# Down-projection with four accumulators instead of seven, its shared products summed in PSUM

## The reference

```python
    hn2 = rmsnorm(x, norm2_g[l])
    up, ffn_new = causal_dwconv(hn2 @ w_up[l], st_ffn[l], ffn_conv_w[l])
    a_f, b_f = jnp.split(up, [D_FF], axis=-1)
    x = x + (jax.nn.silu(a_f) * b_f) @ w_down[l]
y = rmsnorm(x, norm_f_g)
```

## Time and profile before

| | us |
|---|---|
| median of 3 runs | 3172.16 (3170.81 to 3173.29) |
| the profiled execution | 3174.32 |
| its span, first to last instruction | 3172.60 |
| PE busy in the span | 3123.2 |
| DVE busy | 2001.3 |
| ACT busy | 833.6 |
| POOL busy | 449.6 |

### The profile page before, as it was taken

The page is one execution under the profiler, slowest core; times in us unless marked ns, Lnnn a source line. Parts: engine busy times, 40 slices in busy tenths (PEclk is TensorE's granted clock), DMA queues, the critical chain, the costliest instruction groups (busy, mean ns, idle before and its releaser), DMA issues.

```text
span 3172.6 us, 52117 instructions
## 1 busy us (share of the span) xinstructions
PE 3123.2 (98%) x20321; PEld 2020.7 (64%) x20321; DVE 2001.3 (63%) x4791; ACT 833.6 (26%) x1743; POOL 449.6 (14%) x823
## 2 busy tenths in 40 slices
PE   7999999999999999998999999999999999999998
PEld 4555555555555555544877777777776777776675
DVE  2566666666555666666466665656776666666668
ACT  2223333322332233334212112121231122222113
POOL 1000000000000000003421211111163111111110
PEclk9999999999999999999999999999999999999999
DMA  7022222222222222228411111111233111111102
GB/s 249 28 68 87 88 87 68 87 87 74 74 70 71 82 87 88 70 67 242 148 40 50 44 40 40 40 44 50 97 111 95 40 40 40 40 40 48 46 27 80
DMA packets 223169, 236.08 MB, mean 74 GB/s; under 512 B 14204, under 2 KB 167332, under 8 KB 222931
## 3 DMA queue, kind: packets, MB, share of 16 engines
q1 hardware_dynamic: 222931, 232.81, 23.6%
HBM read 203.10 MB, written 29.67 MB: 73 GB/s over the span
## 4 chain that ended last, share of the span: by engine, by line
PE 51%; DVE 1%; ACT 0%; issue 0%; DVEq 0%
PE mlp_bank L2244 34%; PE mlp_bank L2318 15%; PE mlp_bank L2332 2%; PE mlp_bank L2324 0%; DVE mcv L2693 0%; DVE arena L2657 0%; DVE acc L2754 0%; DVE arena L2658 0%; PE mlp_bank L2343 0%; ACT raw L2436 0%; PE mlp_bank L2330 0%; DVE mcv L2697 0%; ACT mcv L2407 0%; DVE raw L2637 0%; DVE raw L2625 0%
## 5 line engine op out<-in xcount | busy, mean ns | idle before, releaser
L727 PE MATMUL mixer_bank<-arena,hnt 128*128 128x451 f32 x2048 | 869.3, 554 | 9.8 <-DMA arena<-in_w_in_dram 9.0
L2244 PE MATMUL mlp_bank<-arena,ws 128*128 128x256 f32 (+1 forms) x2816 | 648.2, 383 | 4.1 <-DVE raw L2631 3.7
L2244 PEld LDWEIGHTS mlp_bank<-arena,ws 128*128 128x128 f32 x2816 | 535.9, 190 | 87.7 <-DVE raw L2631 4.6
L727 PEld LDWEIGHTS mixer_bank<-arena,hnt 128*128 128x128 f32 x2048 | 364.4, 190 | 296.2 <-issue 288.9
L2318 PE MATMUL mlp_bank<-arena 128*128 128x512 f32 x1120 | 495.0, 593 | 0.0
L2726 DVE TENSOR_TENSOR acc<-acc,mlp_bank 128x512 f32<-128x512 f32 x560 | 370.8, 685 | 56.2 <-PE mlp_bank L2318 55.4
L2318 PEld LDWEIGHTS mlp_bank<-arena 128*128 128x128 f32 x1120 | 213.4, 191 | 235.2 <-issue 207.2
L2693 DVE SCALAR_TENSOR_TENSOR mcv<-raw,cf,mcv 128x512 f32<-128x512 f32 (+2 forms) x352 | 266.4, 772 | 50.3 <-ACT mcv L2407 41.5
L2244 PE MATMUL mlp_bank<-arena 128*128 128x256 f32 (+1 forms) x1056 | 247.0, 384 | 2.4 <-PEq L2836 1.4
L767 PE MATMUL mixer_bank<-wo,th 128*128 128x512 f32 x512 | 245.6, 603 | 3.0 <-DMA wo<-in_w_out_dram 2.4
L2244 PE MATMUL mlp_bank<-arena,wu 128*128 128x256 f32 (+1 forms) x1056 | 246.0, 383 | 0.9 <-ACT raw L2436 0.9
(11 more groups left out here) (387 smaller groups left out, 3392.7 us busy)
## 6 DMA issues: line engine op xcount, KB each, us to landing
wo<-in_w_out_dram SPq DMA_DIRECT2D x260, 256.0 KB, 2.9
arena<-in_w_up_dram SPq DMA_DIRECT2D x44, 512.0 KB, 5.0
wu<-in_w_up_dram SPq DMA_DIRECT2D x44, 512.0 KB, 4.9
arena<-in_w_down_dram SPq DMA_DIRECT2D x40, 512.0 KB, 4.2
arena<-in_w_in_dram SPq DMA_DIRECT2D x7, 1804.0 KB, 16.3
xc<-in_x_t_dram SPq DMA_DIRECT2D x16, 512.0 KB, 4.0
xt<-in_x_prompt_dram SPq DMA_DIRECT2D x16, 512.0 KB, 5.2
xr<-in_x_prompt_dram SPq DMA_DIRECT2D x16, 512.0 KB, 3.6
```

What stands on the lines that cost most here:

```text
L727: x = pe.matmul(bank[ring(g)][0:N, 0:GW], hnt[:, k, 0:N], w[:, k, g * GW:(g + 1) * GW], start=(k == 0), stop=(k == KT - 1))
L2244: x = pe.matmul(out[:, 0:N], left[:, k, :], xb[:, slot, k, g * N:(g + 1) * N], start=first and k == 0, stop=k == HK - 1, skip_group_check= ...
```

## The change

There are four accumulators, `acc[:, 0..3, q, :]`, one for each quarter of the output, loaded with the residual. The seven products of a `q` are made in another order and for two `q` in turn: m = 0, 1 and 3 start a bank, m = 2, 4 and 6 add to the bank of m = 0, and m = 5 adds to that of m = 3; DVE adds the bank's content to the accumulator `TARGET[m]` after each. So POOL's `start` and DVE's `combine` are gone, with their semaphores. The closing's products are made in the same scheme: all 28 in pass 0, and in pass 1 the first 14 (tiles 0, 1, 4, 5), the other four tiles and the sample tile staying plain. The closing's weights, weight sums and activation sums have buffers of their own; the weights are loaded near the start of the pass, their sums are made inside the last up-projection, and the activation sums (`last_acts`) on DVE after the last activation.

```diff
-        CLOSING = (16, 18)
+        CLOSING = (28, 24)
+        TARGET = (0, 0, 1, 3, 3, 1, 2)
-        acc = sb("acc", [C, 7, 4, 512])
+        acc = sb("acc", [C, 4, 4, 512])
+        wd_last = [sb(f"wd_last{i}", [C, D])[:, :] for i in range(2)]
+        last_wd_sums = sb("last_wd_sums", [C, 4, 512])
+        last_act_sums = sb("last_act_sums", [C, 3, 512])
-        wd_last = [wu[1][:, i, :, :].rearrange("p k n -> p (k n)") for i in range(2)]
...
+        def tile_out(ps, k):
+
+            if k < 4:
+                return 11 + k
+            return 14 + (2 * (k - 4) + 2 if ps else (11, 13, 12, 14)[k - 4])
...
             def loop(ps):
                 up(ps, 3, 1)
+                if ps:
+                    sp.wait_ge(s_down_done, Q0[1])
+                for p in range(2):
+                    r0 = (2 * PAIRS - 2 + p) * C
+                    sp.dma_start(wd_last[p], w_down[r0:r0 + C, :]).then_inc(s_last_loaded, 16)
...
-                sp.wait_ge(s_m3, group(ps, FT, 0))
-                for p in range(2):
-                    r0 = (2 * PAIRS - 2 + p) * C
-                    sp.dma_start(wd_last[p], w_down[r0:r0 + C, :]).then_inc(s_last_loaded, 16)
...
+            def products(ps, i, a0, a1, asum, wd, wsum, first, last):
+                for o in range(first, last):
+                    m, j = divmod(o % 14, 2)
+                    q = 2 * (o // 14) + j
...
+                    new = m in (0, 1, 3)
+                    bank_free(ps, i, o)
+                    pe.matmul(bank[4 + o % 4][:, :], left, right, start=new, stop=True,
+                              skip_group_check=not new).then_inc(s_down_done, 1)
...
             def close(ps):
...
                 pe.wait_ge(s_act_made, group(ps, FT - 1, 1))
                 pe.wait_ge(s_last_loaded, 32 * (ps + 1))
-                for k, t in enumerate(ORDER + (8,) * ps):
-                    if k == 2:
-                        pe.wait_ge(s_act_made, group(ps, FT - 1, PASSES[ps][1]))
+                products(ps, i, a0, a1, last_act_sums, wd_last, last_wd_sums, 0, 4)
+                pe.wait_ge(s_last_weights, ps + 1)
+                pe.wait_ge(s_last_acts, ps + 1)
+                products(ps, i, a0, a1, last_act_sums, wd_last, last_wd_sums, 4, 14)
+                if ps == 0:
+                    products(ps, i, a0, a1, last_act_sums, wd_last, last_wd_sums, 14, 28)
+                    return
+                turn_tails(0)
+                o = 14
+                for k, t in enumerate(ORDER[4:] + (8,)):
...
-            def start(ps):
-                if ps:
-                    gp.wait_ge(s_combined, 21 * ps)
-                for m in (1, 6, 7):
-                    x = gp.memset(acc[:, m - 1, :, :], 0.0)
-                x.then_inc(s_acc_step, 1)
-                gp.wait_ge(s_acc_loaded, 64 + 96 * ps)
-                gp.wait_ge(s_acc_step, ps + 1)
-                for q in range(4):
-                    x = gp.tensor_tensor(acc[:, 2, q, :], acc[:, 2, q, :], acc[:, 4, q, :], ALU.subtract)
-                x.then_inc(s_acc_ready, 1)
...
-                if ps:
-                    start(ps)
-                    weight_sums(ps, 3, 1)
-                else:
-                    weight_sums(ps, 3, 1)
-                    start(ps)
+                weight_sums(ps, 3, 1)
...
+            def act_terms(a0, a1, sums, n, s_step, step, s_made):
+                lo, hi = slice(0, n), slice(512, 512 + n)
+                dve.tensor_tensor(sums[:, 0, lo], a0[:, hi], a1[:, hi], ALU.add).then_inc(s_step, 1)
+                dve.wait_ge(s_step, step + 1)
+                dve.tensor_tensor(a0[:, hi], a0[:, lo], a0[:, hi], ALU.subtract).then_inc(s_step, 1)
+                dve.tensor_tensor(sums[:, 1, lo], sums[:, 0, lo], a0[:, lo], ALU.subtract).then_inc(s_step, 1)
+                dve.wait_ge(s_step, step + 3)
+                dve.tensor_tensor(sums[:, 2, lo], a1[:, lo], sums[:, 1, lo], ALU.subtract).then_inc(s_made, 1)
...
+            def last_acts(ps):
+                a = 2 * ((PAIRS - 1) % 2)
+                dve.wait_ge(s_act_made, group(ps, FT - 1, 2))
+                if ps:
+                    dve.wait_ge(s_down_done, Q0[1])
+                act_terms(act_[a], act_[a + 1], last_act_sums, 256 if ps else 512, s_last_step, 5 * ps + 2, s_last_acts)
...
+            def add_product(ps, i, o):
+                n = first_out(ps, i)
+                m, j = divmod(o % 14, 2)
+                v = acc[:, TARGET[m], 2 * (o // 14) + j, :] if o < 28 else y_parts[:, :]
+                dve.wait_ge(s_down_done, n + o + 1)
+                if m in (1, 4, 5):
+                    dve.wait_ge(s_y_added, n + o - (5 if m == 5 else 1))
+                elif o % 14 == 0 and not (fixed(i, 1) and ps == 0 and o == 0):
+                    dve.wait_ge(s_y_added, n + o)
+                dve.tensor_tensor(v, v, bank[4 + o % 4][:, :], ALU.add).then_inc(s_y_added, 1)
...
             def close(ps):
...
+                last_acts(ps)
+                for o in range(14 if ps else 28):
+                    add_product(ps, PAIRS - 1, o)
+                if ps == 0:
+                    return
```

More of the change, by code:

```diff
@@ L2309, in down @@
                     pe.wait_ge(s_down_sums, 20 * ps + 2 * i + 2)
[L2310 to L2318, removed]
+                products(ps, i, a0, a1, act_sums, wd, wd_sums, 14 * half + first, 14 * half + min(last, 14))
                 if ps and half and last >= 14:
@@ L2358, in close @@
                         bank_free(ps, i, o)
-                        plain(bank[4 + o % 4], 2 * (i % 2), wd_last, t, e, S if t == 8 else C)
+                        plain(bank[4 + o % 4], 2 * p, wd_last, t, e, S if t == 8 else C)
                         o += 1
-                    if ps and k in (1, 3, 5):
-                        turn_tails(k // 2)
+                    if k < 2:
+                        turn_tails(k + 1)
             def pair(ps, i, p):
@@ new lines, in weight_terms, with first, second @@
+            def weight_terms(wd, sums, s_step, step, s_made):
+                lo, hi = slice(0, 512), slice(512, 1024)
+                def first():
+                    dve.tensor_tensor(sums[:, 0, :], wd[0][:, hi], wd[0][:, lo], ALU.subtract).then_inc(s_step, 1)
+                    dve.tensor_tensor(sums[:, 2, :], wd[1][:, hi], wd[0][:, hi], ALU.subtract)
+                def second():
+                    dve.wait_ge(s_step, step + 1)
+                    dve.tensor_tensor(sums[:, 1, :], wd[1][:, hi], sums[:, 0, :], ALU.subtract).then_inc(s_step, 1)
+                    dve.wait_ge(s_step, step + 2)
+                    dve.tensor_tensor(sums[:, 3, :], wd[1][:, lo], sums[:, 1, :], ALU.subtract).then_inc(s_made, 1)
+                return first, second
@@ L2651, in weight_parts, with loaded @@
             def weight_parts(ps, i):
[L2652 to L2655 removed]
+                first, second = weight_terms(wd, wd_sums, s_sums_step, 5 * (10 * ps + i) + 3, s_down_sums)
+                def loaded():
                     dve.wait_ge(s_wd_loaded, 32 * ((PAIRS - 1) * ps + i + 1))
[L2657 to L2658 removed]
@@ L2660, in second @@
[L2660 to L2667 removed]
+                    first()
@@ new lines, in weight_parts, with last_weight_parts, loaded, made @@
+                return (loaded,), (second,)
+            def last_weight_parts(ps):
+                first, second = weight_terms(wd_last, last_wd_sums, s_last_step, 5 * ps, s_last_weights)
+                def loaded():
+                    dve.wait_ge(s_last_loaded, 32 * (ps + 1))
+                    if ps:
+                        dve.wait_ge(s_down_done, Q0[1])
+                    first()
+                def made():
+                    second()
+                return [((), (loaded,)), ((), (made,))]
@@ L2796, in pair @@
                 closing = fixed(i, PAIRS) and i == PAIRS - 1
-                last = up(ps, i, p, 1, combine_parts(ps) if closing else ())
+                last = up(ps, i, p, 1, last_weight_parts(ps) if closing else ())
                 down(ps, i - 1, 1)
```

101 lines of the change are left out of this document (32 added, 69 removed).

## The result

The changed kernel takes 3180.21 us (median of 17 runs, 3176.67 to 3183.26), the kernel before 3172.16 (17 runs beside them, 3168.85 to 3175.12). The ratio is 1.0025, 95% interval [1.0018, 1.0032]: 8.0 us more, between 5.7 and 10.2. That is slower by a little over the 0.2% named in the prediction; the range of 3171.8 to 3182.0 holds it, the predicted 3178.1 lies 2.1 us too low, and its +5.9 us lies inside that interval. The profiled execution took 3179.38 us, span 3177.7.

A forecast was written before the change was run, and what follows sets the result against it. PE, busy 98% of the span, was taken as the bound. The terms -0.9 - 5.8 - 3.4 + 6.6 + 2.9 + 1.7 - 1.7 + 3.6 + 2.9 sum to +5.9 us, giving 3178.1 us, range 3171.8 to 3182.0.

The forecast's parts named there:

- Steady pairs: In the steady pairs of both passes, products and additions stay as many and additions stay covered: 0 us.
- GpSimd's work in pass 0: First pair of pass 0: without GpSimd's clears and subtractions, PE's wait there goes, -0.9 us.
- GpSimd's work in pass 1: First pair of pass 1: without GpSimd's subtractions, the 20.03 us stretch nears the next pair's 13.86, -5.8 us.
- rival E: First pair of pass 1: weight sums keep DVE late, so the 5.8 us aren't gained; +11.7, 3183.9 us, chance 6%.
- Closing of pass 0: Closing of pass 0: 28 products instead of 32, -3.4; PE waits for DVE's sums, +6.6; half clock afterwards, +2.9 us.
- Rival C: Closing of pass 0: GpSimd locks DVE out for whole operations, sums take 6.4 us; +8.1, 3180.3 us, chance 10%.
- Start of pass 1: Start of pass 1: PE waits while ScalarE finishes four late tiles before its first copy, +1.7 us.
- rival A: Start of pass 1: the third wait halves the clock too; +9.2, 3181.4 us, chance 17%.
- Closing of pass 1: Closing of pass 1: 14 half-sized and 16 plain products, -1.7; wait for sums, +3.6; half clock, +2.9 us.
- Rival D: Both closings: the waits are covered and only the gains stay; 3160.4 us, chance 5%.
- The clock: Behind the waits in both closings, PE runs at half clock, costing +2.9 us each (bounds 0 and 3.1 in pass 0).
- Rival B: Behind the closings' waits the clock costs less, one or both drops costing nothing; 3172.3 to 3175.2 us, chance 14%.

The follow-up runs named there:

- covered closing: The changed kernel with both closings reordered: tiles 2 and 3 plain first, then 14 half-sized products, then the other tiles plain; 3166.26 us, ratio 0.9979.
- plain closings: The changed kernel with both closings plain, in the order of the kernel before, without sums of the last weights and activations; 3166.98 us, ratio 0.9984.

## Why the prediction was right or wrong

The mechanism was right and the size 2.1 us too small, a miss that lies inside the measurement's interval. Against the profile from which it was worked out the sum was right to 0.6 us (+5.9 forecast, +5.3 traced); one term of it was sized from a dear execution.

- **Steady pairs, 0**: right. Twelve products still take 10.46 us by their row, and pass 1 from its first pair to its closing takes 714.59 us in both kernels.
- **GpSimd's work in pass 0, -0.9**: -1.2 (the closing of pass 0 starts 1.17 us earlier, counted from the first product; the idle time in a row's brackets, 0.90 here, is a little less than what PE loses).
- **GpSimd's work in pass 1, -5.8**: this is the term that was mis-sized. The changed side is as forecast or better (13.86 us, no wait; rival E falls), and against the first profile the gain is 6.17. The side of before was read from one profile with 20.03 us; three more have 17.20, 18.19 and 17.77. The gain is 3.3 to 4.3 us against these, 4.4 on the mean of four. The working charged this stretch with a long wait and half clock together, which one profile in four has, and then added the sum to the median, as if the profile's surplus of 2.2 us over it lay elsewhere. That part of the surplus lay in this very term is likely but not shown: the mixers vary by more.
- **Closing of pass 0, -3.4 + 6.6 + 2.9**: -3.4 + 6.6 + 2.5. The wait's chain was right link by link. Rival C falls by the held-back sums: GpSimd's load costs the wait 1.39 us, not the 3.6 of whole operations. Three of the four sums took 1.11 to 1.22 us, 0.42 to 0.53 over their quiet 0.69, and GpSimd's first four operations beside them 4.69 / 4 = 1.17, where held back, with additions from PSUM beside them, they take 11.53 / 16 = 0.72. The Trainium skill, "SBUF — State Buffer", section "Who interferes with whom", has the two engines exclude each other for such pairs of operations; the runs agree that these two slow each other, but one of each takes some 1.17 us, between the 0.72 of no exclusion and the 0.69 + 0.72 = 1.41 of a full one.
- **Start of pass 1, +1.7**: 1.83, and at full clock in every trace after; rival A falls by these rows.
- **Closing of pass 1, -1.7 + 3.6 + 2.9**: -1.7 + 3.7 + 3.1 in the first trace, with 1.46 in place of 3.1 in the second. The four sums of 256 columns took 1.68 us, as taken (1.66).
- **Combining on DVE and the loads of the last weights, 0 each**: right; PE waits for neither. Rival D, the gains alone, fails on the closings' waits, which were not covered.
- **The clock, 2.9 each time**: 2.50, 2.58 and 2.55 in three traces behind the long wait, 3.11, 1.46 and 2.96 behind the short one (the third is the kernel with products at the start of pass 1); with GpSimd's sums held back 1.78 and 2.83. So 2.9 was a little high for both. Rival B falls: each wait cost clock in every trace, and the unused products gave 5.7 us back.

With the mean gain of 4.4 and the mean of 2.5 us for the clock of the second closing (so -1.7 + 3.7 + 2.5 = +4.5) the sum is -1.2 - 4.4 + 5.7 + 1.8 + 4.5 = +6.4; with the second profile's gain of 3.3 it is +7.5. Both lie in the interval of 5.7 to 10.2. Which of them is nearer to the mean execution, and whether anything beyond these terms adds to the medians' +8.0, stays open within that interval; the later comparisons say +8.9 and +7.8.

The edit itself wasn't bad: the covered closing shows what it was worth. It has twelve products ahead of the first that needs a late sum, eight plain and four half-sized; the change had four. The kernel before, which needs no such sums, had eight ahead of the first that needs the last activations.

## What to carry to other kernels

When products are saved by sums that must be formed first, count the independent work that lies between the last input and the first product that needs a sum; here four products in that place cost 6.6 us of waiting and 2.5 us of half clock behind it, and an order with twelve there, at two products more in pass 0, left 1.27 us and no half clock, and nothing once GpSimd's sums were held back. If such a wait can't be covered, unused products in it can keep the clock: here they gave back 5.7 us. Before a term is read as "this stretch takes longer than its neighbour", look at a second profile of the same kernel: a stretch with a wait and half a clock may be a dear draw (20.03 us here, against 17.20 to 18.19 in three more profiles), and the gain is then sized too large.

## What the runs showed of the hardware that was not expected

The same wait of the same kernel doesn't always cost the clock. A wait of 2.84 us was followed by half clock in the first profile of before and by full clock in the third; one of 1.95 us by half clock in the fourth. In the mixers a wait of 1.98 us kept full clock before; half clock follows the same wait of the same code in four of the thirteen traces, as this window of the kernel with plain closings shows:

```profile
68.00:72.00 4.00, 3.30 (x8) 2.06 (x9) 3.90 (x15) 2.53 (x4) 0.00 (x0) 0.60 0.05 11
```

So the prediction's bound of "some 2 us" for rival A was no bound. The waits of 3.5 and of 5.0 to 6.4 us were followed by half clock in each of the four traces named above, with 1.46 to 3.11 us lost. The Trainium skill, "TensorE: Matmul & The Clock Gate", section "What's actually happening", says that the moment at which the clock rises to full speed varies between runs of one kernel; the profiles agree (behind the wait of 3.48 us the loss is 3.11 us in one and 1.46 in another), and show that whether it falls at all varies too.

GpSimd's load adds about the same to a DVE sum whatever its width: 0.42 to 0.53 us on 0.69 for 512 columns, 0.24 to 0.54 on 0.42 for 256. So halving the sums didn't halve what the load cost; holding the GpSimd work back by one wait did away with it.
